# Dense feed-forward: 17 instead of 12 of 22 pairs by seven block products, with weight sums by accumulating DMA and products chained in PSUM

## The reference

```python
def swiglu(h, w_gate, w_up, w_down):
    return (jax.nn.silu(h @ w_gate) * (h @ w_up)) @ w_down
...
x = x + swiglu(h, ffn_w_gate[j], ffn_w_up[j], ffn_w_down[j])
```

## Time and profile before

| | |
|---|---|
| median of 3 runs | 1552.4 us |
| lowest and highest run | 1552.14 and 1553.08 us |
| span of the profiled execution (first to last instruction) | 1550.1 us |
| median less that span (launch and end around it) | 2.3 us |
| PE busy | 1529.5 us (99%), 8392 matmuls |
| DVE busy | 1099.5 us (71%) |
| ACT busy | 872.2 us (56%) |
| POOL busy | 333.7 us (22%) |
| DMA moved | 265.8 MB, mean 171 GB/s |
| mean granted TensorE clock | 0.998 |

### The profile page before, as it was taken

The page is one execution under the profiler, slowest core; times in us unless marked ns, Lnnn a source line. Parts: engine busy times, 40 slices in busy tenths (PEclk is TensorE's granted clock), DMA queues, the critical chain, the costliest instruction groups (busy, mean ns, idle before and its releaser), DMA issues.

```text
span 1550.1 us, 24600 instructions
## 1 busy us (share of the span) xinstructions
PE 1529.5 (99%) x8392; PEld 1321.4 (85%) x8393; DVE 1099.5 (71%) x1784; ACT 872.2 (56%) x1418; POOL 333.7 (22%) x350
## 2 busy tenths in 40 slices
PE   8999999999999999999999999999999999999997
PEld 6888888888999988887888888879898888889895
DVE  7657765758989963436657766776676998887587
ACT  5436665335445442224347764565576888886564
POOL 0204564003544600002015662010000011110000
PEclk9999999999999999999999999999999999999999
DMA  6732212242453233336322112519777999997773
GB/s 221 205 99 69 64 66 82 83 149 84 161 182 131 89 123 91 98 105 153 108 78 80 59 63 88 190 65 327 254 254 256 364 383 373 391 376 267 239 257 132
DMA packets 89793, 265.79 MB, mean 171 GB/s; under 512 B 12497, under 2 KB 22737, under 8 KB 89680
## 3 DMA queue, kind: packets, MB, share of 16 engines
q1 hardware_dynamic: 82864, 248.59, 47.0%
q0 software_dynamic: 6816, 15.74, 3.5%
HBM read 242.84 MB, written 19.83 MB: 169 GB/s over the span
## 4 chain that ended last, share of the span: by engine, by line
PE 93%; DVE 3%; ACT 1%; DMA 1%; issue 1%; SPq 0%; DVEq 0%; ACTq 0%; POOLq 0%
PE ps L1978 14%; PE ps L1983 14%; PE ps L1979 14%; PE ps L2384 8%; PE ps L2359 5%; PE ps L2361 5%; PE ps L2360 5%; PE ps L2386 3%; PE ps L2264 2%; PE ps L2265 2%; PE ps L2272 2%; PE ps L2145 2%; PE ps L2233 2%; PE ps L2234 2%; PE ps L2238 2%; PE ps L2178 1%
## 5 line engine op out<-in xcount | busy, mean ns | idle before, releaser
L973 ACT ACTIVATE w_hi<-raw 128x1024 fp32r<-128x1024 f32 (+1 forms) x124 | 129.3, 1043 | 214.2 <-PE ps L1983 211.1
L1978 PE MATMUL ps<-h_hi,w_hi 128*128 128x512 f32 x544 | 219.9, 404 | 1.0 <-DVE h_lo L1395 0.6
L1979 PE MATMUL ps<-h_lo,w_hi 128*128 128x512 f32 x544 | 212.9, 391 | 0.0
L1983 PE MATMUL ps<-h_hi,w_lo 128*128 128x512 f32 x544 | 212.7, 391 | 0.0
L1375 DVE TENSOR_TENSOR m_lo<-m_raw,m_hi 128x1024 fp32r<-128x1024 f32 x144 | 167.9, 1191 | 58.8 <-ACT m_hi L1016 50.9
L1370 DVE TENSOR_TENSOR w_lo<-raw,w_hi 128x1024 fp32r<-128x1024 f32 (+1 forms) x94 | 112.9, 1201 | 101.6 <-ACT w_hi L973 96.7
L1016 ACT ACTIVATE m_hi<-m_raw 128x1024 fp32r<-128x1024 f32 x144 | 145.3, 1031 | 54.2 <-PE ps L2358 25.9
L2384 PE MATMUL ps<-xt,m_hi 128*128 128x320 f32 x592 | 154.3, 347 | 0.3 <-issue 0.3
L2386 PE MATMUL ps<-xt,m_lo 128*128 128x160 f32 x592 | 140.3, 237 | 0.0
L1983 PEld LDWEIGHTS ps<-h_hi,w_lo 128*128 128x128 f32 x544 | 102.1, 188 | 22.4
L1375 DVE TENSOR_TENSOR m_lo<-h_rows,m_hi 128x1024 fp32r<-128x1024 f32 (+1 forms) x96 | 102.0, 1087 | 22.1 <-ACT m_hi L1016 21.7
(11 more groups left out here) (371 smaller groups left out, 4066.9 us busy)
## 6 DMA issues: line engine op xcount, KB each, us to landing
m_raw<-moe_g SPq DMA_DIRECT2D x88, 512.0 KB, 5.4
raw<-w_in SPq DMA_DIRECT2D x68, 512.0 KB, 3.3
m_raw<-moe_down SPq DMA_DIRECT2D x56, 512.0 KB, 5.7
raw<-w_gu SPq DMA_DIRECT2D x44, 512.0 KB, 3.9
h_rows<-moe_g SPq DMA_DIRECT2D x32, 512.0 KB, 5.1
h_rows<-moe_g SPq DMA_DIRECT2D x32, 384.0 KB, 4.7
h_rows<-moe_down SPq DMA_DIRECT2D x24, 512.0 KB, 5.6
m_raw<-moe_g SPq DMA_DIRECT2D x24, 384.0 KB, 5.4
```

What stands on the lines that cost most here:

```text
L973: A.activation(split_of(n, 0, cols)[0], raw[:, n % RAW, 0:cols], ACT.Copy).then_inc(hi_ready, 1)
L1978: E.matmul(ps[:, bank, :], wh, hi, start=first, stop=False)
L1979: E.matmul(ps[:, bank, :], wh, lo, start=False, stop=False)
L1983: return E.matmul(ps[:, bank, :], wl, hi, start=False, stop=final)
```

## The change

- `SEVENS` becomes `list(range(PLAIN, KF - 2))`: pairs 3 to 19 without a gap, 17 of 22. Before the next unit the place in the ring is rounded up to an even one.
- The order of the products and some signs change, so that products 0, 2, 4 and 6 all go to one place of PSUM and product 3 stands beside: product 2 is accumulated onto product 0's result, 4 onto that, 6 onto that. Products 1 and 5 go to the two halves of a third bank. Before 2, 4 and 6 TensorE waits for ScalarE's copy of the sum so far (`seven_kept`). Plain units now use banks 3 and 7.
- Of the weight sums GpSimd adds one (`sums_ready`); three are made by DMAs that it issues with `accum_op=ALU.add`, which read the weights from DRAM again and add them to what lies in SBUF, 128 x 512 float32 each. The first goes onto the up unit's lower half in its raw buffer (`s1_added`), the second onto the gate's lower half once product 0's low part has been split from it (`s3_added`), the third onto the sum of product 2 once that has been split (`s4_added`). There are three sum buffers, one per pair in turn.
- VectorE makes all low parts, and two additions per pair instead of four. The last steps of pair f (silu, product, high and low part) are done one by one during the first products of pair f + 1.
- The semaphores `x_in` and `y_back` become one set, `block_in`.

```diff
-        SEVENS = [f for f in range(PLAIN, KF - 2) if (f - PLAIN) % 3 < 2]
+        SEVENS = list(range(PLAIN, KF - 2))
@@ job_slots
+                at += at % 2 if kind == "unit" else 0
@@ seven_weights
-            return ((gate, low), (None, 1), (None, 2), (None, 0), (gate, high), (up, high), (None, 2))[j]
+            return ((gate, low), (gate, high), (None, 0), (up, low), (gate, low), (None, 0), (up, high))[j]
@@ seven_bank
+            b = 4 * (SEVENS.index(f) % 2)
+            if j in (1, 5):
+                return ps[:, b + 2, 0:HALF_T] if j == 1 else ps[:, b + 2, HALF_T:T]
+            return ps[:, b + (1 if j == 3 else 0), 0:HALF_T]
@@ SP, load
                     if f in SEVENS:
                         sp.wait_ge(seven_lo, low_by(f))
-                        sp.wait_ge(seven_lo_pool, SEVENS.index(f) + 1)
@@ GpSimd, in place of weight_sums and low_on_pool; called in turn for each q
+            def first_sums(q):
...
+                pool.wait_ge(raw_full[(n + 1) % RAW], 16 * ((n + 1) // RAW + 1))
+                pool.dma_start(up[:, 0:T], w_gu[2 * f + 1][:, T:UNIT], accum_op=ALU.add).then_inc(s1_added, 16)
+                pool.wait_ge(raw_full[n % RAW], 16 * (n // RAW + 1))
+                if q >= len(sums):
+                    pool.wait_ge(seven_lo, LOW_COUNT[JOB[("seven", SEVENS[q - len(sums)], 5)]])
+                pool.wait_ge(s1_added, 16 * (q + 1))
+                pool.tensor_tensor(sums[q % len(sums)][:], up[:, 0:T], gate[:, 0:T], ALU.add).then_inc(sums_ready, 1)
+
+            def later_sums(q):
...
+                pool.wait_ge(sums_ready, q + 1)
+                pool.wait_ge(seven_lo, LOW_COUNT[JOB[("seven", f, 0)]])
+                pool.dma_start(raw[:, (FFN_START + 2 * f) % RAW, 0:T], w_gu[2 * f + 1][:, 0:T], accum_op=ALU.add).then_inc(s3_added, 16)
+                pool.wait_ge(seven_lo, LOW_COUNT[JOB[("seven", f, 2)]])
+                pool.dma_start(sums[q % len(sums)][:], w_gu[2 * f][:, T:UNIT], accum_op=ALU.add).then_inc(s4_added, 16)
@@ ScalarE, job_high
+                        if kind == "seven" and j == 2:
+                            A.wait_ge(sums_ready, SEVENS.index(f) + 1)
+                        if kind == "seven" and j in (3, 4, 5):
+                            A.wait_ge({3: s1_added, 4: s3_added, 5: s4_added}[j], 16 * (SEVENS.index(f) + 1))
@@ ScalarE, at job x
-                        if kind == "seven" and j == 0:
-                            A.activation(quarters[:, 4 * f, :], seven_bank(f, 0), ACT.Copy).then_inc(p1_kept, 1)
+                        if kind == "seven" and j % 2 == 0:
+                            A.activation(quarters[:, 4 * f + (0, 1, 3, 2)[j // 2], :], seven_bank(f, 0), ACT.Copy).then_inc(seven_kept, 1)
                         for y in FREED_BY[x]:
                             job_high(y)
...
+                        if f - 1 in SEVENS and j == 0:
                             silu(f - 1)
+                        if f - 1 in SEVENS and j == (2 if kind == "seven" else 1):
                             act_hi(f - 1)
@@ VectorE, at job x
                         if kind == "seven" and j == 5:
+                            q = SEVENS.index(f)
+                            V.wait_ge(seven_kept, 4 * q + 3)
+                            V.tensor_tensor(quarters[:, 4 * f + 1:4 * f + 4:2, :], quarters[:, 4 * f + 1:4 * f + 4:2, :],
+                                            twice(seven_bank(f, 3)), ALU.add).then_inc(seven_sums, 1)
+                            V.wait_ge(seven_sums, 2 * q + 1)
+                            V.tensor_tensor(silu_of(f), silu_of(f), ps[:, 4 * (q % 2) + 2, :], ALU.add).then_inc(seven_sums, 1)
                         if kind == "seven" and j == 6:
+                            V.wait_ge(seven_sums, 2 * SEVENS.index(f) + 2)
+                            gate_scaled_in_place(f)
                         for y in FREED_BY[x]:
+                            job_low(y)
...
+                        if f - 1 in SEVENS and j == (1 if kind == "seven" else 0):
+                            gated_up(f - 1)
+                        if f - 1 in SEVENS and j == (3 if kind == "seven" else 1):
                             act_lo(f - 1)
@@ TensorE, block_product
+                        q, out, onto = SEVENS.index(f), seven_bank(f, j), j in (2, 4, 6)
...
+                        if j in (2, 4, 6):
+                            E.wait_ge(seven_kept, 4 * q + j // 2)
...
+                            E.matmul(out, wh[:, at], hi, start=k == 0 and not onto, stop=False, skip_group_check=onto)
```

More of the change, by code:

```diff
@@ L253, in build_kernel @@
         gains_in, small_in = sem("gains_in"), sem("small_in")
-        x_in = [sem(f"x_in{k}") for k in range(KD)]
+        block_in = [sem(f"block_in{k}") for k in range(KD)]
         basics, consts = sem("basics"), sem("consts")
@@ L464, in build_kernel @@
         FREED_BY = {d: [x for x in range(2, len(JOBS)) if frees(x) == d] for d in range(len(JOBS))}
-        def on_pool(x):
-            return JOBS[x][0] == "seven" and JOBS[x][2] == 5
-        LOW_COUNT = [sum(not on_pool(y) for y in range(2, x + 1)) for x in range(len(JOBS))]
+        LOW_COUNT = [max(x - 1, 0) for x in range(len(JOBS))]
         def low_by(f):
@@ L484, in job_full @@
             n, part = (FFN_START + 2 * f + j, slice(0, UNIT)) if kind == "unit" else seven_weights(f, j)
-            return sums[part][:] if n is None else raw[:, n % RAW, part]
+            return sums[SEVENS.index(f) % len(sums)][:] if n is None else raw[:, n % RAW, part]
         def job_split(x):
@@ L782, in weight_sums @@
                 gate, up = raw[:, n % RAW, :], raw[:, (n + 1) % RAW, :]
[L783 to L799, removed]
@@ L833, in _ @@
                     pool.wait_ge(rms_ready, 2)
[L834 to L845, removed]
+                    for q in range(len(SEVENS)):
+                        first_sums(q)
+                        later_sums(q)
             steps = [0]
@@ L1199, in _ @@
                             first_down(FFN_END + x - len(JOBS) + 2)
-                        if kind == "seven" and j == 6 and f + 1 not in SEVENS:
+                        if f - 1 in SEVENS and j == 0:
                             silu(f - 1)
-                            silu(f)
+                        if f - 1 in SEVENS and j == (2 if kind == "seven" else 1):
                             act_hi(f - 1)
-                            act_hi(f)
                         if kind == "unit" and j == 0:
@@ L1641, in _ @@
                             scaled(silu_of(f), pair_banks(f)[0]).then_inc(ffn_scaled, 1)
-                        if kind == "seven":
-                            q, banks = SEVENS.index(f), seven_banks(f)
-                        if kind == "seven" and j == 1:
-                            V.wait_ge(p1_kept, q + 1)
-                            if q % 2:
-                                V.wait_ge(seven_sums, 4 * q)
-                            V.tensor_tensor(quarters[:, 4 * f + 2, :], quarters[:, 4 * f, :], banks[:, 2, :], ALU.add).then_inc(seven_sums, 1)
@@ L1649, in _ @@
-                        if kind == "seven" and j == 3:
-                            V.wait_ge(seven_sums, 4 * q + 1)
-                            V.tensor_tensor(quarters[:, 4 * f + 1:u3_at(f) + 1:u3_at(f) - 4 * f - 1, :], twice(quarters[:, 4 * f + 2, :]),
-                                            banks[:, 4:7:2, :], ALU.add).then_inc(seven_sums, 1)
-                        if kind == "seven" and j == 5:
-                            V.wait_ge(seven_sums, 4 * q + 2)
-                            u3 = quarters[:, u3_at(f), :]
-                            if f + 1 < KF - 2:
-                                V.tensor_tensor(quarters[:, 4 * f + 2:4 * f + 4, :], twice(u3), banks[:, 3:5, :], ALU.add).then_inc(seven_sums, 1)
-                            else:
-                                V.tensor_tensor(quarters[:, 4 * f + 2, :], u3, banks[:, 3, :], ALU.add)
-                                V.tensor_tensor(u3, u3, banks[:, 4, :], ALU.add).then_inc(seven_sums, 1)
+                        if kind == "seven" and j == 5:
+                            q = SEVENS.index(f)
[4 more added lines that the diff above has]
+                            V.tensor_tensor(silu_of(f), silu_of(f), ps[:, 4 * (q % 2) + 2, :], ALU.add).then_inc(seven_sums, 1)
@@ L2223, in whole_unit @@
                     def whole_unit(x, f, j):
-                        if f == 2 or (f > 2 and j == 0):
-                            E.wait_ge(ffn_scaled, 1)
-                        if f > 2:
-                            E.wait_ge(seven_sums, 4 * len([g for g in SEVENS if g <= (f - 2)]))
+                        if f == KF - 2 and j == 0:
+                            E.wait_ge(act_ready, 3)
+                        if f == KF - 1 and j == 0:
+                            E.wait_ge(seven_kept, 4 * len(SEVENS) - 4)
+                            E.wait_ge(seven_sums, 2 * len(SEVENS) - 2)
                         bank = pair_banks(f)[j]
```

106 lines of the change are left out of this document (38 added, 68 removed).

## The result

The changed kernel takes 1596.2 us (median of four runs, 1595.7 to 1600.8), the kernel before beside it 1552.3 (1550.4 to 1553.1): a ratio of 1.029 [1.0275, 1.0310]. The forecast was 1569, in a range of 1548 to 1604: a loss was forecast and came, 2.7 times as large. The profiled execution is the longest of the four, 1600.8 with a span of 1599.0, so it is 48.9 us over the 1550.1 of before, where the medians differ by 43.9.

A forecast was written before the change was run, and what follows sets the result against it. TensorE alone bound the kernel; after the change, a loop through the third sum's DMA would. Pairs of 7.15 + 0.8 + 3.4 = 11.35 us, 1.29 over 10.06, 16 times, minus 4.1, gave +16.5: 1569 us, range 1548 to 1604.

The forecast's parts named there:

- the saving: On TensorE, five plain pairs become pairs by seven, each 0.82 us shorter: 4.1 us off the path.
- may come back: At the first pairs, banks 3 and 7 free some TensorE waits: 0 to 2.3 us possible, 0 taken.
- The round: Loop from third sum's landing through ScalarE and VectorE lists to its next issue: 7.15 us, plus 0.8 GpSimd contention, plus landing.
- Z: The moment the third sum's accumulating DMA, for product 5's weights, lands; list times are counted from it.
- the likeliest case: The loop through the third sum's DMA sets the pair time, 11.35 us against 10.06; 1553 to 1593 us, chance 0.55.
- its signs: TensorE late between products 3 and 6; ScalarE waiting 1 to 2 us for sums; landings 3 to 4.5; pitch 11 to 12.
- L: Time from issue to landing of the third sum's accumulating DMA: 3.4 us taken, at most 2.9 to stay hidden.
- So I add no queue: Zero fill landed by Z + 9.9, when the next accumulation has barely begun moving bytes; no queueing time added.
- The sum of 1556 by that page: Forecast total if the 256 KB DMA landed in the skill page's 2.6 us: about 1556 us.
- All hidden: Rival: landing plus contention of 2.9 us or less hides the DMA loop behind TensorE, 1548.3 us; chance 0.20.
- Hand-over in PSUM: Rival: products 2, 4, 6 wait for ScalarE's copies, some 0.5 us a pair, 1556 us; chance 0.08.
- Much dearer: Rival: accumulating DMA lands after 5.9 us, a pair takes 13.85 us, total 1609 us; chance 0.13.

The follow-up runs named there:

- s34_act: Changed kernel with the second and third weight sums as GpSimd additions and the activations' high and low parts one product later: 1544.7 us, ratio 0.9960.
- s34_pool: Changed kernel with the second and third weight sums made by GpSimd additions, the first still by accumulating DMA: 1553.1 us, ratio 1.001.

## Why the prediction was right in kind and short in size

- **What bounds it, and the saving.** Right. With the waits out of the way (s34_act) the span is 1542.1, 8.0 under before. 4.1 of it are the five pairs. Of the 2.3 at the first pairs that "may come back" 0.8 did: the first three pairs took 33.1 us before, 2.1 over 31.0, and take 31.5, 1.3 over. The rest lies outside the pairs by seven: 1.9 us are gained before the first block product (376.0 before, 374.1 now) and 1.2 after the last plain unit.
- **The round.** Right in place and nearly in each step: ScalarE's list held at high 5, the product of f-1, low 0 to low 2, then the next issue. Forecast 7.15 + 0.8 = 7.95 from Z to the issue, measured 7.86 to 7.87 in the undisturbed rounds. It was the likeliest case. Of its signs, TensorE released by ScalarE's copy came; the wait for the DMA into the sums (s4) was the smaller one (10.2 us against 59.0 for s3), and landings of 3 to 4.5 and a pitch of 11 to 12 did not come.
- **L, the term that failed.** 3.4 us were taken and 5.3 (s4, median) to 6.4 (s3) came. With 5.5 in the round the pitch is 13.35; 2.1 us a pair more than 3.4 are 34 us in all, the miss of 32 in the span (27 in the median). The parts, by the runs: s4 with no s3 DMA ahead of it and the fresh loads long issued lands after 3.8, so 0.4 is the size and the accumulation that the nearest row, a copy of 128 KB, did not have; that alone would have given 7.95 + 3.8 = 11.75 a pair, 1575 us. The other 1.5 is traffic beside it. With the zero fills moved s4 lands after 4.1 though s3 is still ahead of it, and with s3 gone after 3.8 though the fills are still there: either change takes most of the 1.5 away, and the runs don't divide it between the two.
- **"So I add no queue."** This is the sentence that was wrong. It had the fill landed by Z + 9.9. Measured with Z at 451.62, the loads were issued at 455.49 and the fill at 456.35, Z + 4.7, which with a landing of 6.8 us is past the next s4's issue at Z + 7.87. The loads wait for low 6, which GpSimd's own addition pushed back. The earlier trace rows had given 6.1 to 6.4 us for a fill; the start was taken too early.
- **The second round, through s3.** Not in the prediction. Only s4 was followed, because it is the last sum. s3 is issued 1.1 us behind the two fresh loads (469.97 against 468.85), behind whose traffic it lands, and holds ScalarE first. Its landings of over 8 us stand behind all four steps of 14.8 to 15.1 us, once through s3 itself and otherwise through the s4 or the high 5 that follows.
- **The page's price.** The Trainium skill ("DMA: Bandwidth & Descriptors", Anatomy of one DMA, SWDGE path) gives 2.6 us for 256 KB, an estimate. The shortest plain copy here took 2.8, near it; the shortest that adds took 3.6, the usual one twice the figure. The sum of 1556 by that page would have missed most of the loss.
- **The rivals.** All hidden: refuted, the shortest landing was 3.6 where 2.9 was the most that could hide. Hand-over in PSUM: refuted, the copies are late only because the list is held, and s34_pool, with the same hand-over, never waits for one in the stage. "Much dearer", at L of 5.9 and 1609, was nearest in number, but the landing was long by traffic more than by the accumulation.
- **The clock.** Not foreseen: the 0.88 to 0.94 of the stretches goes with the stalls. Products 4 and 5 were put at 2.9 us and took some 4.7 in four rounds, which cost 1.7 us in all at most; holding the clock up gained nothing.

## What to carry to other kernels

A transfer that some engine's in-order list waits for is a link of a loop when its issue waits for that same list. Add up the lists from landing to next issue and the landing under the traffic that will be there at that moment, for each such transfer, not the last one only. Give to the DMA queue the sum that is needed latest, keep the urgent ones on an engine, and send bulk traffic (here zero fills) at a time when nothing is being waited for. A transfer issued just behind bulk loads lands when their traffic lets it (here 8.3 us after the first load): then it is the loads' issue that counts, and an earlier issue of the transfer gained nothing here. Before an operation is moved to shorten a list, look whether it leaves the stretch that counts, and what the wait it removes had been hiding.

## What was unexpected of the hardware

- An accumulating DMA of 256 KB from DRAM into SBUF landed after 3.6 us at best and 3.8 to 4.2 when little ran beside it, against 2.8 to 3.4 for the same transfer as a copy, and its issue took GpSimd 0.86 us against 0.54.
- Behind two fresh loads of 512 KB and a fill it took up to 8.8 us. Issued 1.9 or 1.1 us behind the first load, it landed 8.3 to 8.4 us after that load all the same.
- The granted clock fell to 0.50 after a stall of 3.06 us, and matmuls ran at a pitch of 0.21 us instead of 0.12. Idle matmuls kept it at 1.00 and gained nothing, as TensorE was in the round only at times.
- A GpSimd addition made the VectorE operation beside it 1.78 us instead of 0.68, as the earlier trace rows had it; two such a pair fit into 10.1 us, more did not.
